# Beside mLSTM, the projections advance two steps in a round instead of three

## The reference, cut to what matters

```
h = rmsnorm(x, norm1_g[l]);  u = h @ w_in[l]            # 1024 -> 3592 columns
(mq, mk, mv, mo, mi, mf, aq, ak, av, hq, hf, hi, hg) = split(u)
y_m = mlstm_mixer(mq, mk, mv, mo, mi, mf, ...)          # 4 heads, chunkwise, gates, norm
y_a = diff_attention(aq, ak, av, ...)                   # 4 heads, two softmaxes each
y_h = hgrn2_mixer(hq, hf, hi, hg, ...)                  # 4 heads, chunkwise decay
x = x + concat(y_m, y_a, y_h) @ w_out[l]
x = x + square(relu(rmsnorm(x) @ w_up[l])) @ w_down[l]
```

## Time and profile before

| | us |
|---|---|
| median of three runs | 3763.12 |
| profiled execution, own time | 3763.62 |
| its span | 3762.3 |
| PE busy in the span | 3440.9 (91%) |
| DVE, ACT, POOL busy | 1340.2, 1133.7, 1221.5 |
| mean granted TensorE clock | 0.938 of full |

### The profile page before, as it was taken

The page is one execution under the profiler, slowest core; times in us unless marked ns, Lnnn a source line. Parts: engine busy times, 40 slices in busy tenths (PEclk is TensorE's granted clock), DMA queues, the critical chain, the costliest instruction groups (busy, mean ns, idle before and its releaser), DMA issues.

```text
span 3762.3 us, 37110 instructions
## 1 busy us (share of the span) xinstructions
PE 3440.9 (91%) x15602; PEld 2736.4 (73%) x15602; DVE 1340.2 (36%) x2144; ACT 1133.7 (30%) x1553; POOL 1221.5 (32%) x300
## 2 busy tenths in 40 slices
PE   7887899998977999999998789998999978769999
PEld 5654588886745788888886678887888866647887
DVE  4436541224256431222125541124221253573122
ACT  2234342322234432322223232223222232422222
POOL 4210044443300234444442334433444431014442
PEclk9987799999977899999999899999999999879999
DMA  3210033232200132333322223333433332013332
GB/s 118 63 52 1 12 101 101 90 101 68 68 30 1 57 101 90 101 90 92 108 82 80 87 68 93 98 95 112 129 95 97 87 105 85 1 39 91 100 97 72
DMA packets 462183, 296.77 MB, mean 79 GB/s; under 512 B 14330, under 2 KB 454192, under 8 KB 462016
## 3 DMA queue, kind: packets, MB, share of 16 engines
q1 hardware_dynamic: 453664, 277.09, 25.3%
q10 hardware_dynamic: 8352, 17.30, 1.3%
HBM read 285.97 MB, written 8.39 MB: 78 GB/s over the span
## 4 chain that ended last, share of the span: by engine, by line
PE 82%; DVE 13%; ACT 3%; issue 1%; POOL 0%; SPq 0%; DMA 0%; ACTq 0%; DVEq 0%
PE bank L473 24%; PE bank L474 24%; PE bank L475 24%; PE bank L313 9%; DVE x L778 1%; DVE ta L776 1%; DVE ta L539 1%; DVE ta L1160 1%; DVE xl L801 1%; POOL wlo L413 0%; DVE qkv L1950 0%; DVE ta L1947 0%; DVE sqacc L795 0%; DVE scr L1705 0%; DVE tb L1948 0%
## 5 line engine op out<-in xcount | busy, mean ns | idle before, releaser
L413 POOL TENSOR_TENSOR wlo<-raw,whi 128x2048 fp32r<-128x2048 f32 (+3 forms) x288 | 1209.2, 4199 | 2505.9 <-ACT whi L406 2505.9
L473 PE MATMUL bank<-xh,whi 128*128 128x512 f32 x2432 | 972.5, 400 | 69.3 <-DVE xl L801 38.3
L474 PE MATMUL bank<-xl,whi 128*128 128x512 f32 x2432 | 958.8, 394 | 0.0
L475 PE MATMUL bank<-xh,wlo 128*128 128x512 f32 x2432 | 958.1, 394 | 0.0
L406 ACT ACTIVATE whi<-raw 128x2048 fp32r<-128x2048 f32 (+3 forms) x288 | 503.6, 1749 | 685.3 <-PE bank L475 650.4
L473 PEld LDWEIGHTS bank<-xh,whi 128*128 128x128 f32 x2432 | 464.7, 191 | 186.0 <-POOL wlo L413 33.1
L475 PEld LDWEIGHTS bank<-xh,wlo 128*128 128x128 f32 x2432 | 463.4, 191 | 99.0
L474 PEld LDWEIGHTS bank<-xl,whi 128*128 128x128 f32 x2432 | 464.9, 191 | 93.2
L473 PE MATMUL bank<-ah,whi 128*128 128x512 f32 x1216 | 473.0, 389 | 0.0
L474 PE MATMUL bank<-al,whi 128*128 128x512 f32 x1216 | 473.0, 389 | 0.0
L475 PE MATMUL bank<-ah,wlo 128*128 128x512 f32 x1216 | 473.0, 389 | 0.0
(11 more groups left out here) (339 smaller groups left out, 3032.2 us busy)
## 6 DMA issues: line engine op xcount, KB each, us to landing
raw<-in_ffn_w_gate SPq DMA_DIRECT2D x88, 512.0 KB, 4.0
raw<-in_ffn_w_up SPq DMA_DIRECT2D x88, 512.0 KB, 5.3
raw<-in_w_up SPq DMA_DIRECT2D x64, 512.0 KB, 4.8
raw<-in_w_down SPq DMA_DIRECT2D x64, 512.0 KB, 4.9
raw<-in_w_in SPq DMA_DIRECT2D x56, 512.0 KB, 4.8
raw<-in_ffn_w_down SPq DMA_DIRECT2D x64, 384.0 KB, 4.0
raw<-in_ffn_w_down SPq DMA_DIRECT2D x64, 320.0 KB, 3.5
raw<-in_w_out SPq DMA_DIRECT2D x16, 512.0 KB, 4.4
```

Of the source, the lines that this page charges most:

```text
L413: g.e.tensor_tensor(self.wlo[slot][:, 0:n], self.raw[slot][:, 0:n], self.whi[slot][:, 0:n].bitcast(F32), ALU.subtract).then_inc(self.lo_ma ...
L473: pe.e.matmul(bank, hi[:, at:at + P], xh, start=k == ks[0], stop=False)
L474: pe.e.matmul(bank, hi[:, at:at + P], xl, start=False, stop=False)
L475: last = pe.e.matmul(bank, lo[:, at:at + P], xh, start=False, stop=k == ks[-1])
```

## The change

The number of projection steps per round in the second line goes from 3 to 2. It does so on PE, DVE and ACT at once and in both layers, because all of them take their order from this line. No instruction is added or removed.

```
         def second_line():
-            yield from every(3, rest)
+            yield from every(2, rest)
             line = states()
             while not self.diff_begun:
                 yield next(line)
```

## The result

| | before | after |
|---|---|---|
| median, us | 3759.85 (6 runs, 3759.39 to 3765.01) | 3776.80 (6 runs, 3773.26 to 3777.82) |
| profiled execution, own time | 3763.62 | 3776.84 |
| its span | 3762.3 | 3775.5 |
| PE busy in the span | 3440.9 | 3452.3 |
| mean granted clock | 0.938 | 0.938 |

The kernel is slower: the ratio of after to before is 1.0041, 95% interval [1.0029, 1.0053]. That is 16.9 us between the medians, 11 to 20 by the interval; the two profiled executions stand 13.2 us apart. Of the 3.7 us between these two differences nearly all is that the profiled execution of before took 3.8 us more than its median.

What follows compares the result with a forecast made beforehand. The prediction took PE as the bound, losing time where it waits or runs at its lower clock. Seven terms summed to +3.0 us a layer, +6.0 in all: 3769 against 3763.1, with 8 in 10 for 3740 to 3802.

Steps and rivals of the forecast that it cites:

- rival C: Table loads come out as hgrn alternates with the heads, seven of 1.28 us: +4.1 us a layer, 3777; chance 0.06.
- Term 1: Rounds 0 to 9: DVE's second convolution no longer overlaps a POOL pass; -3.5 us a layer.
- Term 2: Rounds 9 to 53: 44 rounds lose one projection step each and mLSTM's cover suffices; -28.9 us a layer.
- Term 3: Rounds 53 to 76, mLSTM's end and `diff`: projection steps replace hgrn's first steps, with some waits; +3.0 us a layer.
- Term 4: Rounds 76 to 80: heads 1 and 3 open alone beside eight projection steps; +10.5 us a layer.
- Term 5: Rounds 80 to 158, heads' stretch: hgrn's first 23 steps come in, its norm and some `out` leave; -4.9 us a layer.
- Term 6: Rounds 158 to 174: hgrn's end runs alone after the last head step; +21.4 us a layer.
- 7, `out`: All 64 steps of `out` come after hgrn, five more than before, starting at 1.2 GHz; +5.4 us a layer.
- rival D: mLSTM's cover tears at two steps a round, so rounds 9 to 53 save only 8.1 us: 3811; chance 0.04.
- rival B: DVE becomes the bound in rounds 80 to 158: 9.1 us more a layer, 3787 in all; chance 0.26.
- rival A: The heads' stretch hides hgrn's start, PE alone counting: 7.9 us less a layer, 3753 in all; chance 0.28.

Runs made afterwards that it cites:

- e10: Same kernel as e2 timed again on another chip (two projection steps a round, six hgrn steps in five rounds): 3742.57 us, ratio 0.9937 to before.
- e2: The change, with hgrn and `out` giving six steps in five rounds beside heads 0 and 2: 3739.30 us, ratio 0.9943 to before.
- e5: Kernel before with two projection steps a round to the 128th, then four, and six hgrn steps in five rounds: 3766.90 us, ratio 1.0003.
- e6: The change, with hgrn and `out` giving four steps in three rounds: 3764.78 us, ratio 0.9996 to before.
- e11: The change, with hgrn and `out` giving five steps in four rounds: 3764.83 us, ratio 0.9995 to before.
- e8: Kernel before, three projection steps a round, with heads 0 and 2 starting four rounds after heads 1 and 3: 3759.96 us, ratio 0.9981.
- e1: The change in layer 0 alone, three projection steps a round kept in layer 1: 3767.41 us, ratio 1.0013 to before.
- e13: The change, with heads 0 and 2 starting eight rounds after heads 1 and 3 instead of four: 3780.83 us, ratio 1.0044 to before.

## Why the prediction was right or wrong

The forecast was 3769, +6 us; measured is 3776.8, +13 in the profiled execution and +17 between the medians, inside the range and on the side that had the most chance. The loss is about twice what the sum gave, and rival C, whose cause did not come in, gave 3777. By the terms, layer 0:

| term | forecast | measured |
|---|---|---|
| 1, rounds 0 to 9 | -3.5 | -3.9 (L1074 at 117.55, before 121.44) |
| 2, rounds 9 to 53 | -28.9 | -29.4 (95.5 against 124.9) |
| 3, rounds 53 to 76 | +3.0 | +1.9 (51.9 against 50.0) |
| 4, rounds 76 to 80 | +10.5 | +14.2 |
| 5, heads' stretch | -4.9 | -6.0 (150.2 against 156.2) |
| 6, lone end | +21.4 | +22.0 |
| 7, `out` | +5.4 | +6.3 (46.5 against 40.2, to the first projection step behind `out`: 497.76 and 492.69) |
| sum | +3.0 | +5.1 |

**Term 1.** The second convolution lost its long pass. DVE's timeline after, and POOL's:

```profile
103.52 2.32 DVE L1160 SCALAR_TENSOR_TENSOR ta<-u,cols,ta 128x511 f32<-128x511 f32 x3
```

```profile
113.90 4.50 POOL L413 TENSOR_TENSOR wlo<-raw,whi 128x2048 fp32r<-128x2048 f32 x1 [22.99 <-ACT whi L406]
```

POOL's pass comes after the four convolutions, all of which take 2.32 us, where it stretched one to 6.56 before. The mechanism was right, and the Trainium skill's rule that the second SBUF input shares an interface with GpSimd (VectorE: DVE Perf Modes, Two Vector instructions with no wait between them) agrees with both traces.

**Term 2.** PE is busy 95.45 of 95.50 us at 0.97: the cover holds and rival D is out. The last "below" stands at 206.36 us, 31.8 earlier than in the earlier trace rows.

**Term 3.** The clock is 1.00, as predicted. PE's waits before the sums on L958's squares are 2.97 and 1.45 us, the second with 1.66 ahead of it for the last mix; I had put 3.3 and 4.0. They are covered slightly better than I worked out. In layer 1 the same 2.97 us wait was followed by 3.4 us at the lower level.

**Term 4** is the one that was mis-sized most, by 3.7 us. It was 8 projection steps at full clock and 5.1 us for the heads' part. PE waited 1.10 us at the heads' start, and the steps behind it ran at the lower level. PE's timeline after:

```profile
264.88 2.79 PE L313 MATMUL bank<-tb,sel 16*128 16x512 f32 x4 [1.10 <-DVE tiny L1344]
267.60 0.80 PE L473 MATMUL bank<-xh,whi 128*128 128x512 f32 x1
268.19 0.63 PE L474 MATMUL bank<-xl,whi 128*128 128x512 f32 x1
...
274.77 0.39 PE L474 MATMUL bank<-xl,whi 128*128 128x512 f32 x1
```

The 128x512 matmuls take 0.63 us there and 0.39 from 274.8 us on. The first twelve follow one another in 0.43 us where at full clock it is 0.23, 2.4 us more. Most of the other 1.3 us is between 277.88 and 279.08: six small matmuls of the heads and a wait of 0.49 us, which the term left out. 8 x 0.68 us was a price at full clock, and nothing in the sum allowed for a fall after one short wait. Nor is the fall the change's own. In layer 1 of e10 the steps and the waits up to here are the same, and the clock stays up:

```profile
1064.81 1.98 PE L319 MATMUL bank<-tb,sel 16*128 16x512 f32 x4 [1.10 <-DVE tiny L1350]
1066.71 0.50 PE L479 MATMUL bank<-xh,whi 128*128 128x512 f32 x1
1067.05 0.40 PE L480 MATMUL bank<-xl,whi 128*128 128x512 f32 x1
```

So 2.4 of the 3.7 us depend on the execution, and the order doesn't tell them.

**Term 5** was right in size. PE is busy 110.93 of 150.20 us and DVE 101.46, which is 68%, below the 80% from which rival B decides. DVE did not become the bound, and hgrn's opening among the heads costs less than the two engines' sum; it does not hide as in rival A, which had 143.4. In the forecast 19.7 us came in, and 18.6 did by the same count. Of the 18.6 PE's busy time brought 13.6 and its idle time 5.0, by the same parts taken out; I had 11.8 and 7.9. The waits changed their names. From the heads' start to `out` PE waits 11.8 us for hgrn's copies on L1705 and 3.2 for L1460 after the change. Before it waited 15.0 us for L1460 and 8.3 for L1705 from 246.3 us on, where hgrn's first levels lay, 5.0 of them among the heads. Waits of PE between 264.9 and 451.5 us after:

```profile
PE bank L313 <- DVE scr L1705: 11.8, 6, 3.0
PE bank L313 <- ACT u L1523: 8.9, 5, 2.7
PE bank L313 <- DVE u L1441: 5.5, 3, 3.5
PE bank L1391 <- DVE u L1460: 3.2, 3, 1.3
```

**Term 6.** hgrn's end is alone and PE is busy 10.65 of 22.00 us; I had said under a third and it is nearly a half. The 9.2 us of PE that term 5 had for this norm, over 21.4 us, should have told me so. Its chain in PE's timeline after:

```profile
436.61 3.54 PE L313 MATMUL bank<-scr,const 128*4 128x512 f32 x4 [1.96 <-ACT scr L958]
...
443.50 3.78 PE L313 MATMUL bank<-scr,sel 4*128 4x512 f32 x4 [0.77 <-DVE scr L1018]
451.53 0.77 PE L473 MATMUL bank<-mh,whi 128*128 128x512 f32 x1 [4.25 <-DVE ml L1289]
```

**Rival C.** Between 98 and 508 us ACT loads its tables 21 times, one of them (L692) after the end of `out`, and 20 times before. They moved from hgrn's L1769 to the heads, as these groups of ACT after show:

```profile
L1515 ACT ACT_TABLE_LOAD x4 | 5.1, 1283 | 0.1
L1533 ACT ACT_TABLE_LOAD x3 | 3.8, 1283 | 0.1
```

There are no more of them, so neither 1.283 us each nor the higher price of a switch that the Trainium skill gives (ScalarE: Activation LUTs, What ACT_TABLE_LOAD costs) comes in.

**What is left.** In layer 0 term 4 missed by +3.7 us, terms 6 and 7 by +0.6 and +0.9, and terms 1, 2, 3 and 5 by -0.4, -0.5, -1.1 and -1.1: together the 2.1 us between forecast and sum. Layer 1 lost 6.2 and not 5.1, mostly since the heads start 30.2 us earlier there and not 31.5; behind the first wait of term 3 its clock was down for 3.4 us. That each term counts twice was a reading of one window. Before the change, heads to `out` took 144.6 us in layer 0 and 141.7 in layer 1 already, so single layers differ by more than the sum gave. 1.9 us lie outside the stage, and I have no row for them; e2 and e10, the same order, differ by 6.9 us in their profiled spans, so a single pair of profiles can't settle such a rest.

**What the sum had right for too simple a reason.** It treated the clock in the heads' stretch as given and moved work between stretches. The paces show that the stretch from the heads to `out` has a term of its own, up to some 15 us a layer, for how often PE gets its higher level. In the change the mean clock was 0.71 to 0.74 where before had 0.74 and 0.75, so the forecast fitted. That was luck: the sum would have failed for e2, as my expectations for e5 and e6 did. Shown is that the same matmuls with nearly the same idle time take 9.5 and 10.6 us less in e10 than in e11, and 13.5 and 12.0 less in e2 than in e11. Why that order keeps the clock is not: I know of no row that tells it ahead, and the guesses that I tested (any pace that takes the lone end away, an offset of the pairs) don't hold in general.

**The best version** is six steps in five rounds with two projection steps a round: 3739.30 and 3742.57 us on two chips, ratios 0.9943 and 0.9937 to the kernel before. The change paid only with this second edit. Of the other orders only e8, three steps a round with an offset, was faster than before.

## What to carry to other kernels

A filler that is spread thinner covers more of the stage that lacks work, but the line behind it starts later, and the end of the longest line then stands alone; count both ends in rounds before touching the number. Here 31.5 us were won ahead of the heads and 36.5 lost behind them, and a pace for the late line of one extra step in five rounds won 37 us. Where small matmuls wait often, try some neighbouring orders on the chip and compare PE's busy time over the same instruction count: here a difference there was the clock, and no sum of waits would have found it. One execution can mislead, so compare medians too.

## What the runs showed of the hardware that I had not expected

- About 696 matmul records from the heads' start to `out` in layer 0 took 134.2 and 135.3 us of PE in e11 and in the change, at mean clocks of 0.72 and 0.71, and 120.7 and 124.7 us in e2 and e10, one order in two executions, at 0.79 and 0.77. The idle time between them was 44.5, 51.4, 45.3 and 45.3 us.
- A wait does not tell whether the clock falls. Thirteen layers in after, e1 (layer 0), e2, e6, e10, e11 and e13 have the same steps up to the heads and the same waits of PE before them: 2.97, 1.66, 1.4 to 1.7 and 1.10 us. Behind the 1.10 us the clock went to its lower level for 6.8 us in four of these layers, for 3.4 in five, and not at all in four. Around the 2.97 us it was 6.8 us in two, 3.4 in five, and not at all in six. In layer 0 of e2 and e10, where the level was down for 6.8 us there, the heads start 3.1 us later than in the change. e6 kept its clock up at the heads in both layers and still had 0.71 and 0.75 in the stretch behind.
- Which level PE gets differs between executions of one kernel too. e2's five runs took 3737 to 3747 us. Its median still held over two chips to 0.1%, and the four medians of e2, e10, e6 and e11 keep six in five apart from its neighbours by 0.5 to 0.6%.
